# A hybrid transformer layer: the borders of the MLA projections and token halves in the feed-forward

## What is computed

```
hn = rmsnorm(x) * scale + shift              # scale, shift from the conditioning vector
p  = hn @ w_in                               # split: q_lat 512, kv_lat 256, rope keys 64, ...
q  = (rmsnorm(q_lat) * g) @ w_uq             # MLA: 6 heads of 128 + 64 rope columns
k, v = (rmsnorm(kv_lat) * g) @ w_uk, @ w_uv
mla  = softmax(q k^T) v                      # over 768 keys
mlstm, na = ...                              # two more mixers; their gates come from p
h  = x + gate * (concat(mla, mlstm, na) @ w_out)
u  = dwconv(rmsnorm(h) * scale + shift @ w_up);  a, b = split(u)
h  = h + gate * ((silu(a) * b) @ w_down)
out = rmsnorm(h) * g
```

## Time and profile before

| | us |
|---|---|
| runs | 2825.7, 2828.6, 2834.2; median 2828.6 |
| profiled execution, its own time | 2836.0 |
| its span | 2834.4 |
| TensorE busy (matmul) | 2717.9, 96% |
| VectorE busy | 1201.2, 42% |
| ScalarE busy | 741.5, 26% |
| GpSimd busy | 193.4, 7% |
| mean granted clock of TensorE | 0.977 of full speed |

### The profile page before, as it was taken

How to read it: one execution, slowest core, us unless ns; L and a number is a source line. 1 busy time by engine, 2 the same in 40 slices (tenths; PEclk the granted TensorE clock), 3 DMA queues, 4 the chain that set the end, 5 groups by cost and what they waited for, 6 DMA issues and landing times.

```text
span 2834.4 us, 31067 instructions
## 1 busy us (share of the span) xinstructions
PE 2717.9 (96%) x12122; PEld 2088.3 (74%) x12122; DVE 1201.2 (42%) x1220; ACT 741.5 (26%) x818; POOL 193.4 (7%) x197
## 2 busy tenths in 40 slices
PE   5999999999999997998999999999999999999996
PEld 3788888887544444786788888888888888888785
DVE  5535533661623367334444333344334433334334
ACT  3222111222223224122323212223122322222221
POOL 1000000100024245000000000000000000000000
PEclk9999999999979999999999999999999999999998
DMA  9765555873160432422222232222232222322222
GB/s 358 283 245 200 200 202 206 317 279 134 37 144 15 131 89 68 166 89 89 74 90 103 81 101 100 104 89 77 100 105 95 97 90 92 104 100 89 84 83 100
DMA packets 97692, 369.04 MB, mean 130 GB/s; under 512 B 21712, under 2 KB 35072, under 8 KB 67128
## 3 DMA queue, kind: packets, MB, share of 16 engines
q1 hardware_dynamic: 72752, 278.26, 29.0%
q0 software_dynamic: 10880, 72.55, 6.8%
q10 hardware_dynamic: 14000, 17.44, 1.7%
HBM read 346.48 MB, written 21.74 MB: 130 GB/s over the span
## 4 chain that ended last, share of the span: by engine, by line
PE 58%; DVE 1%; DMA 0%; issue 0%; ACT 0%; DVEq 0%; ACTq 0%
PE f_ps L2020 57%; PE f_ps L2033 1%; DVE h L2009 0%; DMA f_raw<-in_w_out 0%; DMA h<-in_xT 0%; DVE f_lo L1891 0%; DVE f_square_sum L2006 0%; ACT f_hi L1793 0%; DVE h L1908 0%; DVE f_square_sum L1915 0%; ACT f_val L1799 0%; PE f_pn L2066 0%; PE f_pn L2047 0%; ACT f_val L1812 0%; DVE f_val L1899 0%
## 5 line engine op out<-in xcount | busy, mean ns | idle before, releaser
L2020 PE MATMUL f_ps<-x_hi,f_hi 128*128 128x512 f32 x1632 | 641.5, 393 | 9.3 <-DVE f_lo L1891 7.4
L2020 PE MATMUL f_ps<-x_hi,f_lo 128*128 128x512 f32 x1632 | 643.5, 394 | 0.0
L2020 PE MATMUL f_ps<-x_lo,f_hi 128*128 128x512 f32 x1632 | 642.2, 394 | 0.0
L1891 DVE TENSOR_TENSOR f_lo<-f_raw,f_hi 128x2048 fp32r<-128x2048 f32 (+1 forms) x166 | 337.8, 2035 | 110.9 <-ACT f_hi L1793 98.2
L2020 PEld LDWEIGHTS f_ps<-x_hi,f_hi 128*128 128x128 f32 x1632 | 307.9, 189 | 80.0 <-issue 7.5
L1793 ACT ACTIVATE f_hi<-f_raw 128x2048 fp32r<-128x2048 f32 (+1 forms) x167 | 284.2, 1702 | 292.9 <-PE f_ps L2020 285.6
L2020 PEld LDWEIGHTS f_ps<-x_lo,f_hi 128*128 128x128 f32 x1632 | 307.9, 189 | 71.0
L2020 PEld LDWEIGHTS f_ps<-x_hi,f_lo 128*128 128x128 f32 x1632 | 307.7, 189 | 68.6
L2020 PE MATMUL f_ps<-f_u_hi,f_hi 128*128 128x512 f32 x704 | 277.5, 394 | 4.9 <-DVE f_u_lo L1971 4.9
L2020 PE MATMUL f_ps<-f_u_lo,f_hi 128*128 128x512 f32 x704 | 276.7, 393 | 0.0
L2020 PE MATMUL f_ps<-f_u_hi,f_lo 128*128 128x512 f32 x704 | 276.4, 393 | 0.0
(11 more groups left out here) (270 smaller groups left out, 2917.3 us busy)
## 6 DMA issues: line engine op xcount, KB each, us to landing
f_raw<-in_w_up SPq DMA_DIRECT2D x88, 1024.0 KB, 4.7
i_ring<-in_ada_rest POOLq DMA_DIRECT2D x64, 1024.0 KB, 5.2
f_raw<-in_w_down SPq DMA_DIRECT2D x64, 704.0 KB, 4.1
i_raw<-in_w_in SPq DMA_DIRECT2D x38, 1024.0 KB, 4.8
i_ring<-in_ada_first SPq DMA_DIRECT2D x32, 1024.0 KB, 7.4
f_raw<-in_w_out SPq DMA_DIRECT2D x16, 1024.0 KB, 4.8
g_ring<-rrow SPq DMA_DIRECT2D x24, 256.0 KB, 4.0
i_raw<-in_w_first POOLq DMA_DIRECT2D x16, 320.0 KB, 5.2
```

The lines of the kernel that those rows point to most:

```text
L1891: nc.vector.tensor_tensor(w_lo[s][:, 0:kt, :], raw[s][:, 0:kt, :], w_hi[s][:, 0:kt, :].bitcast(F32), ALU.subtract).then_inc(lo_ok, 1)
L2020: mm = nc.tensor.matmul(pt[s][:, :], w[s][:, k, :], v[:, c, :], start=(k == 0 and n == 0), stop=(k == len(slots) - 1 and n == 2))
```

## The change

Borders of the projections: `qg` and the squares of `q_lat` are made in the input stage, by ScalarE before its last tile is read, and VectorE adds the four squares there to one tile (`sums`); the kv squares are added by VectorE at the start of the projections. The landing of the stores is awaited by SP in the next block, before it clears semaphores and loads `rope`. TensorE's sums have 4 products in place of 16 and 2 in place of 4. The two Exps stand behind the reads of the first two value tiles, the transposes behind the fourth value tile, and SP stores R before em. Some buffers lie elsewhere, and the second half of the rope weights on POOL waits for the rope loads.

```
@@ stage_front, scalar
+                    if u == REST - 1:
+                        act.wait_ge(mod_ok, 2)
+                        act.wait_ge(lat["q_ld"], 16)
+                        for k in range(Q_LORA // P):
+                            nc.scalar.activation(lat["qg"][:, k, :], lat["ql"][:, k, :], ACT.Copy, scale=lat["gq"][:, k:k + 1]
+                                                 ).then_inc(lat["qg_ok"], 1)
+                        act.wait_ge(lat["qg_ok"], Q_LORA // P)
+                        nc.scalar.activation(lat["ql"][:, :, :], lat["ql"][:, :, :], ACT.Square).then_inc(lat["sq_ok"], 1)
                     take(act, u)
...
-                act.wait_ge(v_st, 16 * len(VU))
-                for s in range(2):
-                    act.wait_ge(stored[s], 16 * done[s])
@@ stage_mla, sync
+                for e in ends:
+                    sp.wait_ge(*e)
+                for s in spent:
+                    sp.sem_clear(s)
                 sp.dma_start(rope[:, :, :], A["rope"]).then_inc(r_ld, 16)
                 sp.dma_start(ident[:, :], A["ident"]).then_inc(r_ld, 16)
@@ stage_mla, gpsimd
                 for n in range(2):
+                    if n == 1:
+                        pool.wait_ge(r_ld, 160)
@@ stage_mla, scalar
+                    if (kind, n) == ("v", 0):
+                        act.wait_ge(r_ld, 160)
+                        act.wait_ge(m_ok, 1)
+                        nc.scalar.activation(emr[0:4, :], M[0:4, CTX:TOK], ACT.Exp, scale=-1.0).then_inc(em_ok, 1)
+                    if (kind, n) == ("v", 1):
+                        nc.scalar.activation(emr[32:36, :], M[32:36, CTX:TOK][:, ::-1], ACT.Exp, scale=-1.0).then_inc(em_ok, 1)
@@ stage_mla, tensor
+                        pe.wait_ge(qs_ok, QK - 1)
                         for t in range(QT):
+                            mm = nc.tensor.matmul(sum_ps[0][:, t:t + 1], sums[:, t * P:(t + 1) * P], ones[:, 0:1],
+                                                  start=True, stop=True, skip_group_check=True)
+                    if (kind, n) == ("v", KEYT - 3):
+                        pe.wait_ge(c_ok, 4)
```

```
+            def half_products(pe, t, slots, v_hi, v_lo, sums):
+                def one(s, at, bank, done, mid=None):
+                    for k, c in enumerate(slots):
+                        if mid and k == SUM_AT:
+                            mid()
+                        for n, (w, v) in enumerate(((w_hi, v_hi), (w_hi, v_lo), (w_lo, v_hi))):
+                            mm = nc.tensor.matmul(bank[s][:, 0:HALF_T], w[s][:, k, :], v[:, c, at], start=(k == 0 and n == 0),
+                                                  stop=(k == len(slots) - 1 and n == 2))
+                    mm.then_inc(done, 1)
+                for s in range(2):
+                    pe.wait_ge(lo_ok, t + s + 1)
+                    pe.wait_ge(ev_ok, t + s - 1)
+                    one(s, EARLY, pt, half_ok)
+                one(0, LATE, pb, mm_ok, sums)
+                one(1, LATE, pb, mm_ok)
@@ first_pair
+                for n in range(2 * KT):
+                    k, at, _ = item(n)
+                    if n == SUM_AT:
+                        sum_half(pe, 2, LATE, KT + 3)
+                    pe.wait_ge(hl, n + 1)
@@ vector, the norm
+                for n in range(2 * KT):
+                    if n == 2:
+                        add_half(dve, KT - 2, LATE, (mm_ok, KT - 1), 2, ev_ok)
+                    if n == 4:
+                        add_square_half(dve, KT - 2, LATE, KT + 1, KT + 1)
+                    if n == 8:
+                        add_half(dve, KT - 1, LATE, (mm_ok, KT), 2, ev_ok)
+                    if n == 10:
+                        add_square_half(dve, KT - 1, LATE, KT + 2, KT + 2)
+                    if n == 14:
+                        invert(dve, 2, LATE)
+                    normed(n)
+                    if n >= 1:
+                        low(n - 1)
@@ scalar, between the halves
+                act.wait_ge(w_ld[0], 16 * (KT // 2 + 1))
+                act.wait_ge(mm_ok, KT - 1)
+                nc.scalar.activation(w_hi[0][:, :, :], raw[0][:, :, :], ACT.Copy).then_inc(hi_ok, 1)
@@ tensor, the last turn
+                t = down_tile(g, 0)
+                pe.wait_ge(ul_ok, GT * GROUPS - 1)
+                product(pe, t, 0, slots, u_hi, u_lo, late=(ul_ok, GT * GROUPS))
+                product(pe, t + 1, 1, slots, u_hi, u_lo)
@@ vector, the end
+                for n in range(2 * KT):
+                    if n == 1:
+                        add_half(dve, KT - 2, LATE, (mm_ok, t + KT - 1), 5, ev_ok)
...
+                    if n == KT:
+                        invert(dve, 4, LATE)
+                    scaled(n)
```

More of the change, by code:

```diff
@@ L266, in stage_front @@
                 last[e % 2] = (stored[e % 2], 16 * done[e % 2])
+        ends += [(v_st, 16 * len(VU))] + [(stored[s], 16 * done[s]) for s in range(2)]
         with nc.Block() as block:
@@ L577, in _ @@
                                                ALU.mult).then_inc(mod_ok, 1)
+                dve.wait_ge(lat["sq_ok"], 1)
+                for k in range(1, Q_LORA // P):
+                    if k >= 2:
+                        dve.wait_ge(lat["qs_ok"], k - 1)
+                    nc.vector.tensor_tensor(lat["sums"][:, 0:SEQ], lat["ql"][:, 0, :] if k == 1 else lat["sums"][:, 0:SEQ],
+                                            lat["ql"][:, k, :], ALU.add).then_inc(lat["qs_ok"], 1)
             def product(pe, i, s, both):
@@ L731, with stage_mix @@
 ORDER_R = (4, 5, 0, 1, 2, 3)
-def stage_mix(nc, A, sb, ps, sem, proj, vtok, mix, ones, eps, front, spent, lat, early):
+def stage_mix(nc, A, sb, ps, sem, proj, vtok, mix, ones, eps, front, spent, ends, lat, early):
     rrow = nc.dram_tensor("rrow", [2 * ML_H, KEYT, SEQ], F32, kind="Internal").ap()
@@ L1716, in stage_tail, with item @@
         fin = sem("f_final")
+        first_ld = [sem(f"f_first_loaded{n}") for n in range(2)]
+        half_ok = sem("f_early_half_done")
+        read_ok = sem("f_early_half_read")
         stored = sem("f_stored")
         F0 = KT
+        HALF_T = SEQ // 2
+        EARLY, LATE = slice(0, HALF_T), slice(HALF_T, SEQ)
+        SUM_AT = 4
+        def item(n):
+            k, at = n % KT, EARLY if n < KT else LATE
+            return k, at, full[n // 2 % 2][:, HALF_T * (n % 2):HALF_T * (n % 2 + 1)]
         def up_tile(g, j):
@@ L1915, in add_square, with add_half, add_square_half, invert @@
                 nc.vector.tensor_tensor(ssum[:, :], ssum[:, :], sq[s], ALU.add).then_inc(acc, 1)
+            def add_half(dve, m, at, done, group, read):
+                dve.wait_ge(*done)
+                src = (pt if at is EARLY else pb)[m % 2]
+                nc.vector.scalar_tensor_tensor(h[:, m, at], src[:, 0:HALF_T], mod[:, group * KT + m, 0:1], h[:, m, at],
+                                               ALU.mult, ALU.add).then_inc(read, 1)
+            def add_square_half(dve, m, at, squared, summed):
+                dve.wait_ge(sq_ok, squared)
+                dve.wait_ge(acc, summed)
+                nc.vector.tensor_tensor(ssum[:, at], ssum[:, at], sq[m % 2][:, at], ALU.add).then_inc(acc, 1)
+            def invert(dve, n, at):
+                dve.wait_ge(rt, n)
+                nc.vector.reciprocal(rstd[:, at], rstd[:, at]).then_inc(rs, 1)
+                dve.wait_ge(rs, n)
             @block.vector
@@ L1957, in pair @@
+                low(2 * KT - 1)
+                dve.wait_ge(hl, 2 * KT)
+                dve.wait_ge(lo_ok, F0 + 3)
                 def pair(g, j, after):
                     t, n = up_tile(g, j), GT * g + j
[L1959 removed]
+                    opening = isinstance(j, int) and j == 0 and g == 0
+                    if not opening:
                         split_lo(dve, t + 1, 1, KT)
                     outer(dve, g, j, 0)
[L1962 removed]
+                    if not opening:
+                        split_lo(dve, t + 2, 0, after)
```

306 lines of the change are left out of this document (179 added, 127 removed).

## The result

The changed kernel takes 2789.41 us (median of 4 runs, 2787.34 to 2791.05) against 2827.15 us before (4 runs, 2824.73 to 2834.22) on the same chip: ratio 0.9858, 95% interval 0.984 to 0.9876. The forecast was 2783, its range 2772 to 2805. The profiled execution took 2791.05 us, its span 2789.4 us, against 2836.02 and 2834.4.

What follows compares the result with a forecast made beforehand. TensorE, 96% busy, was taken as the bound, so only its idle and slow time could be won. Six terms summed to 51.0 us, 2836.0 to 2785.0; the forecast was set at 2783, range 2772 to 2805.

Steps and rivals of the forecast that it cites:

- A: Before the projections: TensorE returns sooner and sums shrink, but a new wait precedes the third query head; 5.0 us won.
- B: Border between projections and attention: Exps, transposes and stores move earlier, leaving about 1.3 us of wait; 3.5 us won.
- C: Opening of the attention: TensorE's clock at 1.00 instead of 0.50 behind the shorter wait; 18.7 us won.
- Rival 1: The attention still opens at the low clock, so its 18.7 us are not won: 2802 us, chance 0.16.
- D: Feed-forward's norm: last two output tiles cut in token halves, so the next tile starts earlier; 12.7 us won.
- no wait over 1 us between the output tiles and the first up tiles: Sign of being right: TensorE has no wait over 1 us there, at the feed-forward's norm.
- E: Last turn from up to down: first down tile starts without the last `u` slot, covering the 4.9 us wait; 7.0 us won.
- F: Kernel's end: inversion and scaling in token halves, with a last store of half the size; 4.1 us won.
- The base: Starting time: a varying low stretch could spread runs by 8.5 us, so 2783 was taken, not 2777.6 against the median.
- 2: Feed-forward's norm: VectorE in halves needs 1.2 us per item, giving 9 us back: 2792 us, chance 0.10.
- 3: Behind the norm: short waits lower the clock, which lingers in the feed-forward; slower than before, 200 us gives 2883; chance 0.02.
- 4: Border terms are hidden by other waits: A and E give nothing, C holds; 2795 us, chance 0.04.

Runs made afterwards that it cites:

- the reordered run: The changed kernel with ScalarE's reads of the first two query heads and both roots put ahead of Exp and Ln on the gates: 2784.26 us, ratio 0.9819.

## Why the prediction was right, and where it was not

The forecast of 2783 was 6.4 us too low, inside its range of 2772 to 2805, with the likeliest case the true one. Its own account, 2836.0 less 51.0, must be held against the profiled 2791.05: 6.0 too low, and the table says where.

*A, right in the table (5.0, measured 4.6), and most of that is luck.* TensorE came back after 1.60 us, not 1.3. The new wait was 6.2 us, not 5.7, because the gate rows were there at 714.89 (forecast 713.2). It lowered the clock as charged (2.1 lost, 2.5 forecast). That the wait is ScalarE's queue order and nothing deeper is shown by the reordered run, where it vanishes; I had named the order but not seen that the cure was a move of four instructions. What the working did not see is that its starting figure, 725.85, holds 6.8 us at a clock of 0.50, and that this stretch belongs to that one execution. The same place of the program, in the first trace of before and in the second:

```profile
718.60:725.40 6.80, 6.80 (x20) 4.55 (x20) 5.20 (x4) 4.10 (x6) 0.00 (x0) 0.50 0.01 3
```

```profile
713.20:720.00 6.80, 6.80 (x41) 5.11 (x41) 4.53 (x7) 4.94 (x6) 0.01 (x1) 1.00 0.38 108
```

The third head starts 23.8 us after the input stage in the first trace of before, and 20.3 and 20.2 us in the two others with the old borders. From the input stage to the attention those two take 91.0 us, and the six traces with the new borders and the old order on ScalarE 86.6 to 87.9. So A and B together give 3 to 4 us, not the 7.9 of the table, and A alone about 1 (20.2 less some 17.2, less the 2.1 of slow clock). The forecast did not suffer from it, because it subtracts from 2836.0, the time of the same execution.

*B, right (3.5, measured 3.3).* 1.16 us of wait for 1.3.

*C, right (18.7, measured 17.9), and shown to hang on the wait.* Three traces with a wait of 4.79 us have a low spell of 41 us, one with 4.58 us has 30.7, and all nine with 1.16 us have none. Rival 1 (the attention opens low all the same) is out. The transfers do not hold the clock down either: they are as dense in the opening at 1.00 (DMA share 1.08) as in that at 0.50 (0.93). What the runs do not tell is why a spell that ends after 3 to 10 us in the dense stages lasts 31 to 41 in the attention. The sentence of the Trainium skill (TensorE: Matmul & The Clock Gate, section What's actually happening) that activity releases the throttle fares no better than before: in the run with the Exps moved back TensorE was busy in all of the 30.7 us at 0.50. By it C would be worth 2 to 3 us, the measured worth is 14.4 to 17.9.

*The mixers, missed.* I took the stages between attention and feed-forward to be untouched. With output tile 0 they took 227.0 us instead of 222.0. The windows over that whole stage, of before, of before again, of after and of the run with the reads first:

```profile
934.60:1156.60 222.00, 190.96 (x585) 100.76 (x585) 129.38 (x186) 76.10 (x137) 80.36 (x55) 0.97 0.36 106
```

```profile
929.10:1152.90 223.80, 193.44 (x584) 101.04 (x584) 130.01 (x186) 76.10 (x137) 80.84 (x55) 0.95 0.36 105
```

```profile
909.70:1136.60 226.90, 194.72 (x584) 101.56 (x584) 129.34 (x186) 75.98 (x137) 81.18 (x55) 0.95 0.35 104
```

```profile
900.70:1129.90 229.20, 198.04 (x586) 102.94 (x585) 129.52 (x186) 75.99 (x137) 81.29 (x55) 0.93 0.36 103
```

The instructions are the same, TensorE's busy time differs by 7 us and the mean clock by 0.04. In this stage TensorE has some twenty waits of 0.7 to 3.1 us whatever is changed, and behind some of them the clock is at 0.50 for 3 to 14 us; behind which differs from trace to trace. The low time in it was 14.7 us in the first trace of before and 17.1 to 30.7 in the twelve others, the stage 222.0 to 229.2. The three traces whose attention has the 41 us spell have 222.0, 223.9 and 223.7; the nine with the short border have 224.7 to 229.2, 226.6 on average. So some 3 of the 5.0 us go with the change and the rest is the luck of the first trace. The run with the Exps moved back has its spell of 30.7 us in the attention and still 226.3 here, which speaks against the warm clock in the attention as what brings more low stretches; one trace does not settle it, and why they come stays open.

*D, right in sum (12.7, measured 11.4), by luck: two errors cancel.* The step that was mis-sized is "0.92 us a pair": it is 0.79. I subtracted from pitches of the 512-column pair and did not see that VectorE starts the next instruction before the record of the last one ends: records of 0.47 or 0.48 us stand 0.395 apart. 32 items of 0.13 us are 4.2 us. The step that failed is "(POOL splits `w_lo[0]` beside it)": work on another engine was priced at nothing and cost 4.1 us of wait and half of a 3.4 us low stretch, 5.8 in all; the two runs with the split elsewhere and in pieces show that, and my sign "no wait over 1 us between the output tiles and the first up tiles" failed with it. In the trace of before the same split (it starts at 1328.87) ran beside the reciprocal, which reads one tensor and took 3.35 us, as it does at the end of the kernel with POOL idle; the change put it beside instructions that read two. In all six traces that have the halves and the whole split, one `x_lo` starts 0.27 or 0.28 us behind the split and takes 4.51 us. The Trainium skill has this (SBUF — State Buffer, section Who interferes with whom): a VectorE instruction with two inputs in SBUF contends with a GpSimd instruction that reads SBUF, the pair of ports that the two share is an exclusive lock, and the order of issue decides which of them blocks. The traces agree, and show that the lock lasts a whole instruction, to 0.3 us: 4.51 beside 4.50, and with pieces 1.28 to 1.50 each. By the same section a VectorE instruction with a single SBUF input does not contend, outside the two-port modes, and the reciprocal did not. Read beforehand, it would have pointed at the step, and the 4.50 us of the split in the trace of before would have priced it.

*E, right (7.0, measured 7.0).* Undoing it alone costs 6.4 us in the medians and 7.3 in the stretch from the second pair to the end (1461.7 for 1454.4).

*F, too small (4.1, measured 5.6).* Counted from the end of down tile 13 of the last group, the second inversion ended where it should (22.8 us), the scaling too (29.3 for 29.4). The last store took 3.4 us to the end of the span, where I had taken 4.7; that is the mis-sized term, and nearly all of the 1.5.

*The base.* "The changed kernel meets 2785 in all" assumed that the spell in the attention spreads the runs of before. It does not: it is 41 us each time. What spreads them is in part the end of the input stage (699.5 to 703.4 in the traces) and the short low stretches, among them the 3.6 us of the first trace that stand in A.

*The rivals.* 2 (1.2 us per item) and 3 (a lingering low clock behind the norm) did not occur: 0.79 us, and no low clock from 1325 us to TensorE's last product. Of 4, neither half did.

## What to carry to other kernels

A wait of TensorE has two prices, its own length and the slow time behind it, and the second can be some four times the first: look for it in the windows after each wait, and take the border of such a stage first (moving two Exps back brought back 3.4 us of wait and 14.4 of clock). Before work of POOL is called hidden, look at what VectorE runs in the same microseconds: here the one-input reciprocal was a safe neighbour, two-input instructions stood still for the whole of POOL's instruction, and cutting that in four did not help. Price a chain of short instructions by start to start, not by their recorded durations. And read the clock over every stretch that a forecast subtracts from, in two traces of the kernel before where that can be had: a low stretch of one execution is no gain of the change.

## What the runs showed of the hardware that was not expected

- VectorE's two-input instructions and POOL's split exclude each other by whole instructions: 0.47 us became 4.51 beside a 4.50 us split of POOL, and with four pieces of POOL four instructions in turn took 1.28, 1.50, 1.48 and 1.49 us.
- The low spell in the attention has the same length, 41 us, in three traces of two programs with the same 4.79 us wait, and 30.7 us after 4.58.
- Short instructions of VectorE overlap in the records: 0.48 us long, 0.395 apart.
- Unchanged code of the projections ran 6.8 us at 0.50 in one trace and at 1.00 at the same place in two others, 3.6 us apart.
- The last store, of 512 KB, took 3.4 us from VectorE's last instruction to the end of the span; the last one before, of 1024 KB, took 5.1.
